# A two-branch block with a chunked delta rule: the merge's gate products moved in among RWKV's small products

## What is computed

```python
proj = h @ w_in[l]
p_hg, p_rw, p_gate = jnp.split(proj, [HG_COLS, HG_COLS + RW_COLS], axis=-1)
# y_hg from a gated linear recurrence, y_rw from the RWKV-7 recurrence over 8 heads of 64
g_hg, g_rw = jnp.split(p_gate, N_BRANCH, axis=-1)
merged = jax.nn.sigmoid(g_hg) * (o_hg @ w_branch_hg[l]) + jax.nn.sigmoid(g_rw) * (y_rw @ w_branch_rw[l])
out = merged @ w_out[l]
x = layer_norm(DN_ALPHA * x + (1.0 + gate_raw[:, None]) * out, ln_g[l], ln_b[l])
```

## Time and profile before

| | us |
|---|---|
| runs of the kernel before | 4882.94, 4896.03, 4886.04 |
| median | 4886.04 |
| profiled execution, its span | 4886.8 |
| `rwkv`, first and second layer | 444.7 and 443.9 |
| `merge`, first and second layer | 436.7 and 439.7 |

### The profile page before, as it was taken

One profiled execution on the slowest core, in us unless ns is written; L12 is line 12 of the kernel. 1 busy time (PEld: TensorE's weight loads), 2 busy tenths in 40 slices (PEclk: granted clock), 3 DMA queues, 4 the chain that ended last, 5 costly groups with the idle time before them and its releaser, 6 DMA issues. The chain is left out here.

```text
span 4886.8 us, 74327 instructions
## 1 busy us (share of the span) xinstructions
PE 4189.9 (86%) x28756; PEld 2805.5 (57%) x28756; DVE 1754.7 (36%) x2545; ACT 1148.2 (23%) x1583; POOL 702.1 (14%) x490
## 2 busy tenths in 40 slices
PE   6999668779996998577879988888789999999963
PEld 3887646656665887466756664543544444444433
DVE  3453754441413003655533321641241111111128
ACT  1111343321212111433311222530211111111114
POOL 2221010012322220010112220000000100001015
PEclk8999888789998999878989998999799999999985
DMA  5764232402221222101012211011129999999967
GB/s 198 211 192 131 72 120 93 166 32 86 80 79 60 95 94 101 37 24 38 16 63 76 90 47 46 1 37 35 64 94 354 358 357 359 357 358 361 357 247 268
DMA packets 246693, 715.16 MB, mean 146 GB/s; under 512 B 24897, under 2 KB 116546, under 8 KB 210626
## 3 DMA queue, kind: packets, MB, share of 16 engines
q1 hardware_dynamic: 198370, 536.70, 31.5%
q10 hardware_dynamic: 25632, 93.33, 4.7%
q0 software_dynamic: 22464, 81.80, 4.6%
HBM read 584.89 MB, written 126.88 MB: 146 GB/s over the span
## 5 line engine op out<-in xcount | busy, mean ns | idle before, releaser
L434 PE MATMUL ps<-s_proj_hS,s_proj_wS 128*128 128x512 f32 x3216 | 768.0, 402 | 62.4 <-POOL s_proj_wS L324 62.4
L434 PEld LDWEIGHTS ps<-s_proj_hS,s_proj_wS 128*128 128x128 f32 x3216 | 615.1, 192 | 211.4 <-ACT s_proj_wS L384 63.2
L1840 PE MATMUL ps<-s_mix_hS,s_mix_wS 128*128 128x512 f32 x1536 | 394.8, 413 | 40.2 <-POOL s_mix_wS L1699 35.5
L1840 PEld LDWEIGHTS ps<-s_mix_hS,s_mix_wS 128*128 128x128 f32 x1536 | 291.7, 190 | 135.0 <-issue 67.6
L2794 PE MATMUL ps<-s_exp_gu,keep_hT 128*128 128x512 f32 x736 | 341.5, 608 | 16.5 <-DMA s_exp_gu<-in_w_gu_dram 15.0
L2778 PE MATMUL ps<-s_exp_wd,s_exp_aT 128*128 128x512 f32 x736 | 331.2, 593 | 1.9 <-ACT s_exp_aT L2704 1.9
L2799 PE MATMUL ps<-s_exp_gu,keep_hT 128*128 128x512 f32 x736 | 330.9, 592 | 0.0
L1699 POOL TENSOR_TENSOR s_mix_wS<-s_mix_w,s_mix_wS 128x1024 fp32r<-128x1024 f32 x96 | 231.0, 2407 | 580.8 <-ACT s_mix_wS L1708 580.8
L2744 DVE TENSOR_TENSOR s_exp_sg<-s_exp_sg,ps 128x256 f32<-128x256 f32 x92 | 38.7, 421 | 664.2 <-ACT s_exp_sg L2725 664.2
L324 POOL TENSOR_TENSOR s_proj_wS<-s_proj_w,s_proj_wS 128x1024 fp32r<-128x1024 f32 x67 | 178.9, 2672 | 561.0 <-ACT s_proj_wS L384 561.0
L352 DVE COPY s_proj_o<-ps 128x512 f32<-128x512 f32 x66 | 45.6, 690 | 567.3 <-PE ps L434 567.3
(11 more groups left out here) (447 smaller groups left out, 6164.2 us busy)
## 6 DMA issues: line engine op xcount, KB each, us to landing
s_exp_gu<-in_w_gu_dram SPq DMA_DIRECT2D x184, 1024.0 KB, 10.8
s_exp_wd<-in_w_down_dram SPq DMA_DIRECT2D x92, 1024.0 KB, 8.8
yrow<-keep_hT ACTq DMA_DIRECT2D x92, 512.0 KB, 9.6
keep_mix<-in_w_ada_dram SPq DMA_DIRECT2D x80, 512.0 KB, 5.5
s_proj_w<-in_w_in_dram SPq DMA_DIRECT2D x66, 512.0 KB, 4.4
proj<-s_proj_o ACTq DMA_DIRECT2D x66, 512.0 KB, 2.7
yrow<-keep_xT SPq DMA_DIRECT2D x4, 8192.0 KB, 26.0
s_mix_w<-in_w_in_dram SPq DMA_DIRECT2D x64, 512.0 KB, 3.5
```

The costliest lines, as they stand in the source:

```text
L434: mm = pe.matmul(k.ps[:, 6 + half if last else 2 * b + half, :], wS[:, b, x, t, :], hS[:, y, t, half * HALF:(half + 1) * HALF], start=(t = ...
L1840: mm = pe.matmul(k.ps[:, bank, :], wS[:, b, u, x, :], src[:, v, x, :], start=(x == 0 and u + v == 0), stop=(x == KT - 1 and u == 1))
```

## The change

Per layer, the 768 gate products (16 slabs, 2 halves of the tokens, 24 products each) leave `merge` and go into `rwkv` as 64 pieces of 12. A pair of heads gets 16 pieces. Eleven stand between the levels, updates and sums, and one before the scan; in the first and third pair (even `p`) the last four are strewn over the scan in threes and fours (`SCAN_FILL`), in the second and fourth four stand in the gram part instead. The gate product accumulates in PSUM bank 7. So the sums of `rwkv` use one bank at a time (bank 6), in halves of 512 columns, each half with its own wait, and their users on ACT and DVE are cut in halves too.

For each piece SP loads 256 KB of `w_in` into one of two buffers, ACT rounds it (`high`), POOL subtracts (`low`) into a ring of three, and after each second piece ACT takes the bank (`take`) and SP stores 256 KB to `gates`. The modulated `h` comes from a store that `projection` now makes (`hs`, sixteen transfers of 512 KB) and lies in the place of `xT`; the weights lie in the place of `yhg`. So `yhg` is stored and loaded back around them, and `xT` is loaded again in `merge` (in the second layer from `x1`, which `projection` stores).

`merge` is written out without loops. It loads the gates in place of computing them, and has branch products, output products and sums; six of the eight mean sums of a half stand between its output products. The split of `h` is gone. In `rwkv` the key input is loaded earlier, ACT copies a level's product before it takes the next pair's key, and `bonus_terms` stands behind the scan. The four 8 MB transfers to `yrow` go to the attention stage.

```diff
+        self.hG = nc.alloc_sbuf_tensor_at("gate_h", [P, 2, KT, HALF], F32R, offset=at_xT)
+        self.wG = nc.alloc_sbuf_tensor_at("gate_w", [P, RING, 2, KT // 2, P], F32R, offset=at_mix)
+        self.wraw = nc.alloc_sbuf_tensor_at("gate_raw", [P, 2, KT // 2, P], F32, offset=at_mix + RING * T * 4)
...
 TERMS = ((0, 0), (0, 1), (1, 0))
+RING = 3
+NGATE = 2 * KT
+PIECES = 2 * 2 * NGATE
...
+                y, t = (n - KEEP) % 2, (n - KEEP) // 2
+                if 0 <= t < KT:
+                    sp.wait_ge(hhi_ready, t + 1)
+                    if y:
+                        sp.wait_ge(hlo_v, (t + 1) // 2)
+                        sp.wait_ge(hlo_p, t // 2 + 1)
+                    sp.dma_start(k.scratch["hs"][:, :, y, t, :].rearrange("a p n -> p a n"),
+                                 hS[:, y, t].bitcast(F32).rearrange("p (a n) -> p a n", a=2)).then_inc(st_h, 16)
+                elif l and KT <= t < 2 * KT and y == 0:
+                    sp.dma_start(k.scratch["x1"][t - KT], k.xT[:, t - KT]).then_inc(st_x, 16)
+            sp.wait_ge(st_h, 16 * 2 * KT)
...
+    SCAN_FILL = [3, 4, 3, 4, 3, 4, 3, 0, 3, 3, 3, 3, 3, 3, 3, 3]
...
+            def weights(g):
+                if g < PIECES:
+                    u = g // 2
+                    wait(sp, gl_ready, g - 1)
+                    sp.dma_start(wraw[:, g % 2], I["w_in"][l, CG1 + u % NGATE, :, g % 2 * HK:(g % 2 + 1) * HK, :]).then_inc(ld_g[g % 2], 16)
...
+            def keep_gate(u):
+                sp.wait_ge(g_taken, u + 1)
+                sp.dma_start(gates[u // NGATE, u % KT, :, u % NGATE // KT, :], og[:]).then_inc(st_g, 16)
...
+                sp.dma_start(k.scratch["yh"][h], k.yhg[:, h]).then_inc(st_y, 16)
+            modulated(0)
+            sp.wait_ge(st_y, 16 * HG)
+            for g in range(4):
...
+            for u in range(PIECES // 2):
+                p, x = u // (EACH // 2), u % (EACH // 2)
+                weights(2 * u + 4)
+                weights(2 * u + 5)
+                if x == 5 + p % 2 * 2 and p + 2 < PAIRS:
+                    inputs(p + 2)
+                keep_gate(u)
+                if x == p % 2 * 2 and p + 1 < PAIRS:
+                    first_values(p + 1)
+                if x == 1 + p % 2 * 2:
+                    outputs(p)
+                if u == NGATE - 1:
+                    modulated(1)
+            sp.wait_ge(g_done, PIECES)
+            sp.wait_ge(gl_ready, PIECES)
+            for h in range(HG):
+                sp.dma_start(k.yhg[:, h], k.scratch["yh"][h]).then_inc(ld_y, 16)
+            sp.wait_ge(ld_y, 16 * HG)
+            sp.wait_ge(st_g, 16 * (PIECES // 2))
...
+            def low(g):
+                if g < PIECES:
+                    pool.wait_ge(gh_ready, g + 1)
+                    pool.tensor_tensor(wG[:, g % RING, 1], wraw[:, g % 2], wG[:, g % RING, 0], ALU.subtract).then_inc(gl_ready, 1)
...
+            def high(g):
+                if g < PIECES:
+                    act.wait_ge(ld_g[g % 2], 16 * (g // 2 + 1))
+                    wait(act, g_done, g - RING + 1)
+                    act.activation(wG[:, g % RING, 0], wraw[:, g % 2], ACT.Copy).then_inc(gh_ready, 1)
+            def take(u):
+                act.wait_ge(g_done, 2 * u + 2)
+                wait(act, st_g, 16 * u)
+                act.activation(og[:], k.ps[:, 7, :], ACT.Copy).then_inc(g_taken, 1)
...
+                    high(g + 5)
+                    take(u + 1)
+                    g, u = g + 4, u + 2
+                level(p, 0)
+                high(g + 2)
...
+            def piece_part(g, a, z):
+                u, y, n = g // 2, g % 2, 0
+                if a == 0:
+                    pe.wait_ge(gl_ready, g + 1)
+                    if y == 0:
+                        wait(pe, g_taken, u)
+                    if g == 0:
+                        pe.wait_ge(sig_w, 2)
+                    if g % (PIECES // 2) < 2:
+                        pe.wait_ge(ld_h, 16 * KT * (u // NGATE + 1))
+                for t in range(y * HK, (y + 1) * HK):
+                    for w, h in TERMS:
+                        if a <= n < z:
+                            mm = pe.matmul(k.ps[:, 7, :], wG[:, g % RING, w, t - y * HK, :], hG[:, h, t, :],
+                                           start=(t == 0 and w + h == 0), stop=(t == KT - 1 and w == 1))
+                        n += 1
+                if z == n:
+                    mm.then_inc(g_done, 1)
+            def piece(g):
+                piece_part(g, 0, 3 * HK)
...
                 pe.wait_ge(pr_taken, 4 * p + 3)
                 level(p, 0)
+                bonus_sums(p, 0)
+                piece(g)
                 pe.wait_ge(pr_taken, 4 * p + 4)
                 update(p, 0)
+                piece(g + 1)
                 level(p, 1)
+                bonus_sums(p, 1)
+                piece(g + 2)
+                update(p, 1)
                 if more:
-                    pre_decay(p + 1)
-                update(p, 1)
+                    pre_decay(p + 1, 0)
+                piece(g + 3)
...
+                    if p % 2 == 0:
+                        for x in range(sum(SCAN_FILL[:i - 1]), sum(SCAN_FILL[:i])):
+                            piece_part(g + 12 + x // (3 * HK), x % (3 * HK), x % (3 * HK) + 1)
...
+            def branch(m):
+                hf, j, b = m // NJ, m % NJ, m % 2
+                wait(sp, ys_ready, 2 * (m - 1))
+                sp.dma_start(wb[:, b, 0:4], I["w_branch_hg"][l, j]).then_inc(ld_wb[b], 16)
+                sp.dma_start(wb[:, b, 4:8], I["w_branch_rw"][l, j]).then_inc(ld_wb[b], 16)
+                wait(sp, mul_done, m - 1)
+                sp.dma_start(sg[:, b], k.scratch["gates"][hf, j]).then_inc(ld_sg[b], 16)
...
+            def branches(m):
+                hf, b = m // NJ, m % 2
+                wait(pe, m_ready, 2 * (m - 1))
+                pe.wait_ge(ld_wb[b], 32 * (m // 2 + 1))
+                for g, y in enumerate((k.yhg, k.yrw)):
+                    for x in range(4):
+                        mm = pe.matmul(k.ps[:, 2 * b + g, :], wb[:, b, 4 * g + x, :], y[:, x, cut(hf)], start=(x == 0), stop=(x == 3))
+                    mm.then_inc(ys_ready, 1)
...
+                n = (SLOT_BLOCKS - NE_BLOCKS) // NSPARE
+                sp.dma_start(spare[:, p * n + NE_BLOCKS:(p + 1) * n + NE_BLOCKS, :],
+                             k.xT[:, 0:1, :].to_broadcast([P, n, D])).then_inc(st_spare, 16)
+            sp.wait_ge(st_spare, 16 * NSPARE)
```

More of the change, by code:

```diff
@@ L1136, in _ @@
                     key_part(p + 1)
-                level(p, 0)
+                high(g + 3)
+                take(u)
+                level(p, 1)
+                high(g + 4)
                 if more:
@@ L1383, in _ @@
                 for i in range(1, NST + 1):
+                    if i == 3 and more and l:
+                        decayed_b(p + 1)
                     if i == 2:
@@ L1590, in _ @@
                     mm.then_inc(zx_ready, 1)
+                if more:
+                    pre_residual(p + 1, 1)
+                piece(g + 10)
                 pe.wait_ge(zx_a, p + 1)
@@ L1688, in _ @@
-                for i in rounds(sp, NJ // 2):
-                    for b in range(2):
-                        j = i * 2 + b
-                        wait(sp, lo_ready, j + (hf * NQ + 2 * NJ - 1))
-                        sp.dma_start(w[:, b], I["w_out"][l, j]).then_inc(ld_w[b], 16)
+                for j in range(2 if hf == 0 else 4, NJ):
+                    branch(hf * NJ + j)
+                    if j == 4 or j == 5:
+                        slab(hf * NJ + j - 4)
+                for j in range(2, NJ):
+                    slab(hf * NJ + j)
+                    if hf == 0 and j >= 6:
+                        branch(NJ + j - 6)
@@ L1828, in _ @@
+                for j in range(NJ):
+                    merged(hf * NJ + j)
+                    if hf and j == 1:
+                        centre(0)
+                    if hf and j == 5:
+                        normalise(0)
+                for j in range(NJ):
+                    add(hf * NJ + j)
+            centre(1)
             normalise(1)
```

716 lines of the change are left out of this document (415 added, 301 removed).

## The result

The changed kernel takes 4756.63 us, the median of four runs (4743.28 to 4764.35), against 4887.82 for the kernel before in the same rounds (4882.94 to 4896.03): a ratio of 0.9722, with an interval of 0.9703 to 0.9741. The forecast was 4757, so the sum came out. Its terms came out less well: `rwkv` grew by 247 us where 224 were forecast, `merge` shrank by 379 where 357 were. The profiled execution of the changed kernel is the longest of its four runs, with a span of 4762.1.

What follows compares the result with a forecast made beforehand. PE was taken to bound both stages: `merge` by work, `rwkv` by work, handovers and clock. `rwkv` +224, `merge` −357 and elsewhere +4 made −129 on 4886.8, so 4757 us, range 4670 to 4850.

Steps and rivals of the forecast that it cites:

- A piece of 3.0 us: In `rwkv`, twelve gate products cost 2.75 us plus 0.25 for changing from fp32 to fp32r; sixteen cost 48 per pair.
- Pieces fill the handovers: In `rwkv`, a piece of 3.0 us in each handover fills PE's wait for ACT's copy, late by at most 3.4.
- the other instructions go beside PE: In `rwkv`, ACT's roundings, POOL's subtractions and halved sums were taken as 0, bounded by 2 us a pair.
- the fourth pair's stretch without a gap: In `rwkv`, each pair was priced from the fourth pair's warm stretch of 50.6 us at a clock of 0.96.
- The clock: In `rwkv`, pieces keep PE at 2.4 GHz; a granted clock of 0.95 or more was expected.
- The gates' 176.3: In `merge`, removing 32 groups of 24 gate products at 5.5 us each saves 176.3 us per layer.
- the head's 4.1: At the start of `merge`, only a load of 3.6 us stays ahead of PE instead of 7.6, saving 4.1.
- Late weights (1): In `rwkv`, pieces wait for load, rounding and subtraction; at 2 us a piece it costs 256, giving 5013; chance 0.08.
- Clock down (2): In `rwkv`, the granted clock stays near 0.83, costing 168 us and giving 4925; chance 0.05.
- POOL against DVE (3): In `rwkv`, POOL's subtractions block DVE: +38 us, 4795, or 4911 if all on the path; chance of 30 or more 0.15.
- Better than built (4): In `rwkv`, pieces cost 2.75 us and fill 4 more us of waits per pair, giving 4693; chance 0.17.
- Loads in `merge` (5): `merge` without gates becomes bound by DMA, costing some 60 us and giving 4817; chance 0.02.

Runs made afterwards that it cites:

- after_old: The changed kernel with ACT's old order put back at two places of its list; `rwkv` took 559.0 and 562.7 us.
- before_order: The kernel before, with only the next pair's key, decay and rate moved behind level copies in ACT's list; 4837.74 us, ratio 0.9884.

## Why the prediction was right, and where it wasn't

**The sum.** Forecast −129, by the profiled spans −124.7: `rwkv` +128.2 and +119.0 (forecast +106.6 and +117.5), `merge` −187.7 and −191.4 (−178.7 each), all other stages together +7 (+4). Two misses of 23 and 22 us cancel, so that the median meets the forecast within one us is luck; with the same sign they would have made 45, which is still inside the stated range. In the second layer's `rwkv` two more cancel: its pairs are 6.5 over the forecast, its prologue and tail 5.0 under it.

**A piece of 3.0 us** held. **Pieces fill the handovers** held: no wait at L1714 in the changed kernel, nor with ACT's old order (after_old). The forecast took the copy to be late by at most 3.4, from one pair of the first layer, and the earlier trace rows put those 3.4 down to `issue` and not to ACT; that they go with ACT's order came out only by the run before_order. The second layer's last level, late by 6.6 three times, was not looked at. What was wrong is that the other instructions go beside PE and change nothing. Without any gate work the rearranged `rwkv` was 31 and 41 us shorter, and ACT's order makes 25.8 and 24.8 of them. It did no harm to the sum, because each pair was built from the fourth pair's stretch without a gap, which is what remains whether a wait is filled or removed. It matters for the advice: much of what the pieces fill is to be had without them.

**The clock.** Assumed was 2.4 GHz throughout the pairs. They had 0.95, 0.99, 0.89 and 0.95, and the third pair's 0.89 is the largest miss, 13.8 of the 21.6 us by which the first layer's `rwkv` was under-priced. The scans of the second and fourth pair, which get no pieces, were not looked at for this. Another 4.9 is the wait for Kd, in the first pair: POOL's subtractions are queued ahead of the first key, and the forecast priced POOL by its busy time and not by what stands ahead of what.

**`merge`.** The gates' 176.3 and the head's 4.1 held. The misses are the finer wait at the first output products (5.3 us a layer in gaps, and a slow stretch of 3.4 us behind the first gap of the kernel before, worth 1.7) and 1.7 of the stall for weights (2.1 in the second layer): together 8.7 of the 9.0 by which the first layer was off. The second layer's 12.7 has some 3.6 more; there the kernel before has one more stretch at 1.2 GHz, of 6.8 us, which would be worth about that.

**The rivals.** Late weights (1): PE's waits show none for them in either layer (1.5 and 1.0 us in all for the bank that ACT takes), and the chain costs nothing by the run with one product in twelve against the run with none. Clock down (2): no, with 0.94 and 0.96 over the four pairs, though it falls in single stretches. POOL against DVE (3): the lengthening is there, off the path. Better than built (4): no. Loads in `merge` (5): no, one stall of 1.3 us for weights in the first layer.

## What to carry to other kernels

When waits at a handover are to be filled with work from elsewhere, first look at what stands ahead of the awaited instruction in the other engine's list: here three lines moved in ACT's list gave 50 us without any filler. Price a change by runs that leave the moved work out, or two edits that cover the same wait will both claim it. Compare such runs by PE's idle and busy time apart, since the clock moves a stage by more than the wait in question. A forecast that is built from a stretch with no gaps is robust against which of them does it, and not against the clock.

## What was not expected of the hardware

The same kernel has its 1.2 GHz stretches at different places from one execution to the next: the third pair's gram part was slow in the profiled run (281 products in 32 us) and fast in the next (495). That moved a pair by some 13 us, and with it the time: eight runs of the changed kernel lie between 4743 and 4780 us. Filling the gaps with products of constants did not keep the clock up in the fourth pairs, where it fell as the filling began: there they cost 13 and 8 us.
